# POOL adds up seven of eight tiles of the first stack's norms, and TensorE's last sums move behind the next product's first step

## What is computed

```python
h = x
for l in range(2):
    proj = h @ w_in[l]
    mixed = concat(nsa_mixer(...), gla_mixer(...), pool_mixer(...))
    h = layer_norm(ALPHA * h + mixed @ w_out[l], ln1_g[l], ln1_b[l])
    ff = square(relu(h @ w_up[l])) @ w_down[l]
    h = layer_norm(ALPHA * h + ff, ln2_g[l], ln2_b[l])

def layer_norm(x, g, b):
    mu = mean(x, -1)
    var = mean(square(x - mu), -1)
    return (x - mu) * rsqrt(var + 1e-5) * g + b
```

## Time and profile before

| | |
|---|---|
| median of three runs | 1381.71 us (1381.26 to 1381.72) |
| the profiled execution, its own time | 1381.62 us |
| its span in the profile | 1379.8 us |
| PE busy | 1352.9 us, 98% of the span |
| DVE busy | 1037.1 us, 75% |
| ACT busy | 879.2 us, 64% |
| POOL busy | 492.8 us, 36% |
| chain that ended last | PE 78%, DVE 12%, ACT 6% |
| granted PE clock | 0.999 of full on average |

### The profile page before, as it was taken

How to read it: one execution, slowest core, us unless ns; L and a number is a source line. 1 busy time by engine, 2 the same in 40 slices (tenths; PEclk the granted TensorE clock), 3 DMA queues, 4 the chain that set the end, 5 groups by cost and what they waited for, 6 DMA issues and landing times.

```text
span 1379.8 us, 31437 instructions
## 1 busy us (share of the span) xinstructions
PE 1352.9 (98%) x13296; PEld 1160.5 (84%) x13296; DVE 1037.1 (75%) x1465; ACT 879.2 (64%) x1442; POOL 492.8 (36%) x402
## 2 busy tenths in 40 slices
PE   9999999999999999999999999999999999999997
PEld 7778888887778888888778888889888778988887
DVE  6897975569898854568887988756978866898853
ACT  5686764447665863446895755555787888675652
POOL 0143760124146830225210566503114211366610
PEclk9999999999999999999999999999999999999999
DMA  9543566544443656525336365552643334375551
GB/s 366 186 145 132 179 222 211 192 156 156 141 146 139 234 197 214 188 100 172 123 112 225 141 221 189 169 195 93 222 145 123 108 123 148 129 253 207 198 168 32
DMA packets 37020, 234.64 MB, mean 170 GB/s; under 512 B 4752, under 2 KB 7824, under 8 KB 10384
## 3 DMA queue, kind: packets, MB, share of 16 engines
q1 hardware_dynamic: 36880, 232.63, 49.0%
HBM read 231.57 MB, written 1.05 MB: 169 GB/s over the span
## 4 chain that ended last, share of the span: by engine, by line
PE 78%; DVE 12%; ACT 6%; issue 2%; POOL 1%; DMA 1%; SPq 0%; ACTq 0%; DVEq 0%; POOLq 0%
PE psum L744 22%; PE psum L746 22%; PE psum L745 22%; DVE low L2511 4%; PE psum L848 1%; PE psum L850 1%; PE psum L849 1%; PE psum L969 1%; ACT high L1768 1%; ACT m L2219 1%; PE psum L973 1%; POOL h L3414 1%; POOL m L3412 1%; DMA raw<-stream 1%; DVE arena L2666 1%
## 5 line engine op out<-in xcount | busy, mean ns | idle before, releaser
L2511 DVE SCALAR_TENSOR_TENSOR low<-raw,high 128x2048 f16<-128x2048 f32 (+5 forms) x247 | 518.9, 2107 | 180.2 <-ACT high L1768 179.5
L744 PE MATMUL psum<-u,high 128*128 128x256 f16 (+2 forms) x1924 | 529.8, 275 | 0.6 <-ACT arena L1754 0.4
L746 PE MATMUL psum<-u,low 128*128 128x256 f16 (+2 forms) x1924 | 529.5, 275 | 0.0
L745 PE MATMUL psum<-u,high 128*128 128x256 f16 (+2 forms) x1924 | 529.5, 275 | 0.0
L1768 ACT ACTIVATE high<-raw 128x2048 f16<-128x2048 f32 (+4 forms) x248 | 418.2, 1689 | 119.5 <-PE psum L746 89.8
L744 PE MATMUL psum<-arena,high 128*128 128x256 f16 (+3 forms) x1208 | 331.0, 274 | 1.7 <-DVE arena L3111 1.4
L746 PE MATMUL psum<-arena,low 128*128 128x256 f16 (+3 forms) x1208 | 330.9, 274 | 0.0
L745 PE MATMUL psum<-arena,high 128*128 128x256 f16 (+3 forms) x1208 | 330.9, 274 | 0.0
L744 PEld LDWEIGHTS psum<-u,high 128*128 128x128 f16 x1924 | 188.1, 98 | 32.5 <-issue 3.7
L745 PEld LDWEIGHTS psum<-u,high 128*128 128x128 f16 x1924 | 188.3, 98 | 27.9 <-issue 0.7
L746 PEld LDWEIGHTS psum<-u,low 128*128 128x128 f16 x1924 | 188.2, 98 | 27.3
(11 more groups left out here) (382 smaller groups left out, 1903.0 us busy)
## 6 DMA issues: line engine op xcount, KB each, us to landing
raw<-stream SPq DMA_DIRECT2D x206, 1024.0 KB, 4.8
raw<-stream SPq DMA_DIRECT2D x8, 768.0 KB, 4.3
raw<-stream SPq DMA_DIRECT2D x5, 512.0 KB, 4.4
raw<-stream SPq DMA_DIRECT2D x2, 896.0 KB, 4.5
con<-consts SPq DMA_DIRECT2D x1, 1437.0 KB, 12.3
h<-x_t SPq DMA_DIRECT2D x2, 512.0 KB, 6.0
raw<-stream SPq DMA_DIRECT2D x2, 448.0 KB, 5.5
misc<-small SPq DMA_DIRECT2D x1, 512.0 KB, 13.4
```

Source lines behind the costliest of these rows:

```text
L744: pe.matmul(out, w_hi, x[0], start=start, stop=False)
L745: pe.matmul(out, w_hi, x[1], start=False, stop=False)
L746: return pe.matmul(out, w_lo, x[0], start=False, stop=stop)
L2511: tell(dve.scalar_tensor_tensor(low[:, at:at + w], raw[:, off:off + w], W_SCALE, high[:, at:at + w], ALU.mult, ALU.subtract), split_ready ...
```

## The change

`added_up` becomes 7 for norms 0, 1 and 2 and stays 6 for norm 3. POOL therefore adds tiles 1 to 6 and their squares for the first three norms, and waits for each square that it needs. The hook `late` inside the last tile goes away. `finish` now runs `late`'s two sums first, and then those of the tiles that POOL leaves: tile 7 for norms 0 to 2, tiles 6 and 7 for norm 3. The places of `finish` stay.

```diff
         def added_up(m):
 
-            return 6 if m % 2 else 4
+            return 6 if m == 2 * DEPTH - 1 else KT - 1
...
-                            if late and j == tiles - 1 and k == ks_in[3 * kt // 4]:
-                                late()
                             mm = tile(name, step, k, j, rhs, n)
...
-                def sums(t):
-                    pe.wait_ge(*evac_value(first + t))
-                    mean_of(5, m_all[:, t, 0:S], S, False, False)
-                    pe.wait_ge(sq_ready, squares_of(m) + t + 1)
-                    mean_of(4, sq_all[:, t, 0:S], S, False, False)
-
                 def late():
                     pe.wait_ge(ln_acc, m + 1)
                     mean_of(5, root[:, 0:S], S, True, False)
                     mean_of(4, sq_all[:, 0, 0:S], S, True, False)
-                    for t in range(added_up(m), KT - 2):
-                        sums(t)
 
                 def finish():
-                    for t in (KT - 2, KT - 1):
+                    late()
+                    rest = range(added_up(m), KT)
+                    for t in rest:
                         pe.wait_ge(*evac_value(first + t))
                         mm = mean_of(5, m_all[:, t, 0:S], S, False, t == KT - 1)
                     mm.then_inc(mean_done, 1)
-                    for t in (KT - 2, KT - 1):
+                    for t in rest:
                         pe.wait_ge(sq_ready, squares_of(m) + t + 1)
                         mm = mean_of(4, sq_all[:, t, 0:S], S, False, t == KT - 1)
                     mm.then_inc(sums_done, 1)
...
-                        pool.wait_ge(sq_ready, squares_of(m) + (4 if t == 3 else 6))
+                        pool.wait_ge(sq_ready, squares_of(m) + (4 if t == 3 else max(t + 1, 6)))
```

More of the change, by code:

```diff
@@ L929, in last_pair_in_halves, with product @@
                 tile_sums(n, KT - 2, 1)
-            def product(name, rhs, ready, n, after=None, late=None, order=None, pairs=2, begun=0, last_pair=None, awake=0, x_high=None, ready_at=0):
+            def product(name, rhs, ready, n, after=None, order=None, pairs=2, begun=0, last_pair=None, awake=0, x_high=None, ready_at=0):
                 prod = products[name]
                 first, kt, steps = prod["first"], prod["kt"], prod["steps"]
-                tiles = len(prod["widths"])
                 ks_in = order or range(kt)
@@ L1005, in finish @@
                     mm.then_inc(sums_done, 1)
-                return shift, late, finish
+                return shift, finish
             def first_two_pairs():
@@ L1346, in first_layer @@
                 values(5)
-                shift, late, finish = layer_norm(f"out1_{l}", 2 * l)
-                product(f"out1_{l}", lambda k: (g_hi[:, k, :], g_lo[:, k, :]), lambda k: pe.wait_ge(x_ready, 8 * (3 * l + 1) + OUT1_ORDER.index(k) + 1), S, shift, late, OUT1_ORDER, pairs=1)
+                shift, finish = layer_norm(f"out1_{l}", 2 * l)
+                product(f"out1_{l}", lambda k: (g_hi[:, k, :], g_lo[:, k, :]), lambda k: pe.wait_ge(x_ready, 8 * (3 * l + 1) + OUT1_ORDER.index(k) + 1), S, shift, OUT1_ORDER, pairs=1)
                 abreast_raw(f"up1_{l}", 2 * l, finish)
                 product(f"up1_{l}", x_at, operand_ready(3 * l + 2), S, begun=2, ready_at=4)
-                shift, late, finish = layer_norm(f"down1_{l}", 2 * l + 1)
-                product(f"down1_{l}", lambda k: (f1_hi[:, k, :], f1_lo[:, k, :]), lambda k: pe.wait_ge(f_ready, FT1 * l + k + 1), S, shift, late)
+                shift, finish = layer_norm(f"down1_{l}", 2 * l + 1)
+                product(f"down1_{l}", lambda k: (f1_hi[:, k, :], f1_lo[:, k, :]), lambda k: pe.wait_ge(f_ready, FT1 * l + k + 1), S, shift)
                 if l == DEPTH - 1:
```

## The result

| | median | runs |
|---|---|---|
| before | 1381.72 us | 6 runs, 1381.26 to 1382.51 |
| changed | 1389.92 us | 6 runs, 1388.95 to 1390.74 |

The ratio is 1.0059, with a 95% interval of 1.0046 to 1.0072. The change costs 8.2 us. The forecast was +2.85 us, and its range ended at 1386.8.

A forecast was written before the change was run, and what follows sets the result against it. TensorE's queue plus its waits was taken to bound the kernel. Terms 2 x 1.85 (norms 0 and 2) - 0.5 (norm 1) - 0.35 (norm 3) gave +2.85 us, 1384.6; range 1382.6 to 1386.8.

The forecast's parts named there:

- What bounds norms 0 and 2: Ends of the attention/mix products: TensorE waits for POOL's adds behind k = 0, +1.85 us each, bounds +0.6 and +2.1.
- The meeting's price: Norms 0 and 2: each POOL add meeting a DVE splitting operation costs 0.47 us, read from norm 1.
- The rule of the Trainium skill: Two-input VectorE and SBUF-reading GpSimd instructions exclude each other: DVE delayed 3.2 us, not 1.9, by four meetings.
- 0.04 us between tile 7 and PE: Norm 0, kernel before: TensorE reaches the four sums behind k = 0 only 0.04 us after DVE adds tile 7.
- rival 1: TensorE's clock falls in the new waits at norms 0 and 2, about 1.7 us lost per fall; chance 0.27.
- Norm 1: End of the first feed-forward product: two sums fewer, gain partly passed on, -0.5 us, bounds -0.86 and -0.3.
- Norm 3: End of the stack: two sums move behind tile 7, none removed, -0.35 us, bounds -0.5 and 0.
- Rival 2: Norms 0 and 2: POOL and DVE meetings cost less than in norm 1; 1382.1 to 1382.9, not slower; chance 0.11.
- rival 3: Removed sums count in full and the wait does not: 6.0 us faster, 1375.7; chance 0.04.

The follow-up runs named there:

- e1: Changed kernel with 36 dummy matmuls ahead of the wait for POOL at norms 0 and 2, the wait itself kept: 1385.70 us.
- e2: Kernel before with four more POOL adds at norms 0 and 2, into a spare buffer, for which nobody waits: 1383.74 us.
- e3: Changed kernel, but POOL adds only 6 tiles at norms 0 and 2 and TensorE sums tiles 6 and 7 behind k = 0: 1386.23 us.
- e4: Kernel before at norms 0 and 2, with the change at norms 1 and 3 alone: 1381.69 us.
- e7: Changed kernel, but at norms 0 and 2 POOL adds five tiles and the sums stand behind k = 1: 1380.84 us.
- e11: Changed kernel, but POOL adds five tiles, sums behind k = 1 (norms 0 and 2), 16 dummy matmuls, all mean sums ahead of the squares': 1379.93 us.
- e5: Changed kernel, but POOL adds 4 and 6 tiles as in the kernel before; only the sums' move into `finish` remains: 1382.43 us.
- e6: Changed kernel, but at norms 0 and 2 the sums stand behind k = 3 and not k = 0: 1385.98 us.
- e9: Kernel before with 16 dummy matmuls ahead of TensorE's first wait in the second layer's first product: 1381.99 us.

## Why the prediction was wrong, point by point

**What bounds norms 0 and 2: right.** PE waits for POOL behind k = 0, idle 4.14 us (4.3 summed). Tile 6 is 1.0 us late; DVE's four splitting operations take 3.62 us (4 x 0.87 = 3.5 summed); POOL releases 1.85 us behind tile 6 (1.9 summed). With the clock held in e1 the step costs 1.83 us against the 1.85 of the sum. The meeting's price, read from another norm, held: 0.47 us there, and 1.96 us for four in e2. The rule of the Trainium skill (SBUF — State Buffer, "Who interferes with whom") names the right pair of instructions, but taken to the letter it gave 3.2 us for the four; here the trace does not agree, and the measurement decides.

The prediction's 0.04 us between tile 7 and PE is misread: it compares tile 7 with the first of four sums, which is tile 6's. The slack was 0.47 us (e2). Its sum does not use the 0.04, so the 1.85 us stand.

**The clock: the step that failed.** The prediction gave its rival 1 a chance of 0.27 and left it out of the sum. It compared one number with one number: 4.6 us of idleness at the end of the kernel, after which the clock fell, and 4.3 us in the forecast. From a single instance it drew a border between them, and so put the term at nothing. It measured 1.7 us at each of the two norms: norm 0 costs 3.5 us by the starts of the same matmuls, and 1.83 with the clock held in e1. In the changed kernel the clock fell some 4.3 and 4.4 us after the last matmul at the two norms, and in e3 with a longest wait of 1.45 us. How little the single instance said can be read at the same place, the end of the kernel, in the profile of the changed kernel, where the last matmul ends at 1381.51:

```profile
1381.60:1383.60 2.00, 0.00 (x0) 0.00 (x0) 1.57 (x4) 0.56 (x2) 0.00 (x0) 1.00 0.13 39
1383.70:1388.90 5.20, 0.00 (x0) 0.00 (x0) 2.13 (x6) 0.00 (x0) 0.00 (x0) 0.50 0.63 181
```

There it fell 2.2 us into idleness and not 4.6. Over the thirteen profiles of this document the end of the kernel shows everything from 1.9 us (e4) to 4.9 (e2), with the same matmuls ahead of it. Only two of them are longer than 4.3 us (4.6 and 4.9), so the prediction's one instance was a long one by chance, and could carry no border. The price that the rival named, 1.7 us for each, was right. Two falls would have given 1388.0 (the prediction says 1388.1).

**The third fall: missing altogether.** No case of the prediction had the clock fall where PE waits anyway, in the next layer's first product. The stretch there, in the kernel before:

```profile
324.76:328.18 3.42, 1.70 (x16) 1.33 (x15) 2.87 (x3) 3.42 (x6) 0.00 (x0) 1.00 0.04 17
328.18:331.60 3.42, 3.42 (x34) 3.07 (x32) 3.32 (x5) 3.42 (x7) 0.00 (x0) 1.00 0.37 81
```

PE does almost the same in the first of these rows as in the changed kernel's from 328.96, and the clock holds here and falls there. By their times, executions with and without it stand side by side in e1, in e7 and in the kernel before. So the clock at that place is decided anew in each execution, and the work ahead of it seems to change the odds: all six executions of the changed kernel have the mean clock of three falls, while the eleven of e2 form one group (1383.4 to 1384.2) with a clock of 0.998 or 0.999, and its profile has no fall there. What sets the odds stays open.

**Norm 1: too much.** The sum was -0.5. The mean was copied at 307.47, 3.77 us behind the kernel before, where the stretch ahead was 4.3 behind: 0.5 us gained. Then DVE's next step behind the normed operands came at 318.12 instead of 314.02, 4.1 behind, and only 0.2 were left. DVE's copy of the mean, and behind it two rows of PE:

```profile
307.47 0.43 DVE L2592 COPY root<-psum 128x256 f32<-128x256 f32 x1 [0.43 <-PE psum L966]
...
319.90 1.13 PE L1069 MATMUL psum<-arena,misc 16*128 16x256 f32 x4 [0.17 <-ACT arena L1857]
321.56 0.28 PE L744 MATMUL psum<-u,high 128*128 128x256 f16 x1 [0.54 <-DVE low L2502]
```

These are two waits that the kernel before does not have (the same matmuls start at 316.22 and 317.45 there, without idle time). PE ran 0.87 us ahead as far as them and gave 0.66 back in them. So the prediction had the path wrong: it took the wait at 327.43 for the next one, and did not ask whether an earlier arrival would open a new one, on DVE's remainder of a weight slot. What took the 0.3 in DVE's chain was not isolated; POOL's own norm steps run there beside DVE's, and whether they meet otherwise than before is not shown. e4 confirms the size, and in e11, where the mean comes earlier, norm 1 gains more.

**Norm 3: right.** Mean copied at 606.85, root's sum at 604.92; by the starts of the same matmuls ahead of and behind it -0.35 us, as summed.

**The total**, by the starts of the same matmuls in the two profiles: 3.5 at norm 0, -0.1 at norm 1 with the product behind it, 1.7 for the third fall, 3.5 at norm 2, -0.35 at norm 3, 0.2 later, 8.3 us from end to end (the terms are rounded). The profiled executions differ by 0.8 more, at their start; the medians differ by 8.2. Of this the prediction had 2.85 in its sum, 5.0 are three falls of the clock, and most of the rest is what norm 1 did not give.

**The rivals.** Rival 1 came, in full (both waits), and a third fall with it that it did not have. Rival 2 (meetings that cost less) and rival 3 (the removed work counts) are excluded by e2, e5 and e6. What rival 2 described, a delay that fits into DVE's idle time, is what e7 makes with two meetings instead of four.

## What to carry to other kernels

When work is taken off a busy engine, look at what it was waiting beside: here six sums (2.59 us) filled the time until a tile arrived, with 0.47 us to spare, so removing them turned work into a wait. A helper engine's instruction is not free because nobody waits for it: each POOL add that met a DVE operation with two SBUF inputs cost DVE 0.5 us, and the number of adds that fitted was DVE's idle time divided by that (0.9 us, two adds, in e7). A new wait of PE of several microseconds should be priced with the clock falling in it, as the likely case and not as a tail, and old waits further on with it; one observed delay of the fall is no border, so look at the same place in several profiles. Dummy matmuls in a wait that must stay were cheap insurance here (0.2 us for sixteen in e9).

## What the runs showed of the hardware that was not expected

- The granted clock fell to 1.2 GHz not only behind one long wait: in e3 PE had done one sum between waits of 1.45 and 0.42 us before it fell, and at the third fall the one wait ahead of it was 1.78 us, with PE busy on both sides of it.
- Behind the last matmul of the kernel the granted clock fell after 1.9 to 4.9 us, over thirteen profiles in which the same matmuls stand ahead of it.
- With the same instructions in the same order the clock seems to fall in one execution and not in the next: the kernel before had 9 of 33, 7 of 31 and 10 of 27 executions in a group some 1.7 us higher, and 16 dummy matmuls in a wait of 1.7 us removed the group without moving the median (1381.99 against 1381.88).
- A meeting costs DVE 0.47 to 0.5 us each time (1.96 us for four, 1.0 for two), less than the POOL add's own length (0.73 to 0.80 us).
